# A two-block fp32 transformer on one Trainium2 core: row broadcast by memory reload replaced by small matmuls

## The chip, the cores and the metric

The kernel runs on one core of a Trainium2 chip. The metric is the time on the device in microseconds (us), the median of repeated runs; lower is better. Engines are named as in the profile: PE is the matmul engine, DVE the vector engine, ACT the scalar (activation) engine, POOL the general-purpose engine, SP the queue that loads weights.

## The reference, cut to what matters

Input is one sequence of 1024 tokens, 1024 wide, float32. The first block (differential and stick-breaking attention, then a gated FFN with a convolution) is not touched. The second block is touched between its input projection and its output projection:

```python
q_a,k_a,v_a,q_m,k_m,v_m,o_m,i_m,f_m,g_a,g_m = split(h @ w_in)
y_a = sliding_window_attention(rope(q_a), rope(k_a), v_a, sinks)      # 8 heads of 64, window 128
logf = log_sigmoid(f_m + b_f); b = cumsum(logf); ig = i_m + b_i       # mLSTM gates, 4 heads
m_t = max(b + m_prev, max(d_mat))                                     # running maximum, the stabilizer
scores = (q_m @ k_m) * exp(d_mat - m_t)                               # 4 heads of 128
h_m = (scores @ v_m) / max(abs(sum(scores)), exp(-m_t))
y_m = sigmoid(o_m) * head_layer_norm(h_m)
merged = sigmoid(g_a) * (y_a @ w_ba) + sigmoid(g_m) * (y_m @ w_bm)
mix = merged @ w_out
```

For each mLSTM head the kernel needs one row of 1024 numbers, minus the running maximum, repeated on all 128 partitions. Four rows become a 128 x 4096 array, called NEGMB. It also needs two small arrays with time along the partitions (GT and EMT, 128 x 32 each).

## The kernel before, in words

Feature dimension and partitions: activations are stored with 128 features on the partitions and the 1024 tokens along the row, in 8 tiles. Every large product is done in split precision: the activation is split in a high and a low part (`hh`, `hl`), each weight chunk (128 x 1024) too (`wh`, `wl`), and one 128 x 128 x 512 product takes three matmuls (lines 546 to 548). Products of q, k, v and the like are plain float32; the profile shows each as two matmul records.

Weights go through a fixed ring: SP loads a chunk into `raw`, POOL makes `wh` (line 492, a cast) and `wl` (line 494, a subtraction), PE multiplies, and `chunk_done` tells POOL that the slot is free. There are three slots.

The order of the work in the second block is written out by hand for each engine:

1. 23 projection chunks of the input projection. Among them chunk 5 gives the gate rows, from which DVE and ACT make, in `ROW1` and `ROW2` (4 partitions each), the rows of the stabilizer. At n == 8 DVE negates the running maximum (`if_ch` 8); at n == 10 ACT writes it to the memory scratch `m_scratch` (lines 1599 to 1601).
2. Eight gate chunks, m = 8 to 15, first half of the tokens (`gate_product(..., 0)`). ACT copies each result out and stores it. After m = 9 it reloads `m_scratch` into NEGMB, repeated over 128 partitions (line 1621). Ahead of m = 12, PE runs `stabilizer_columns()`, 16 matmuls of 4 rows by 4 columns (lines 975 and 977), which ACT copies into GT and EMT after its copy of m = 12 (lines 1624 and 1625).
3. The mLSTM steps, s = 0 to 7: `m_scores` (line 1015), `m_values` (line 1027), with DVE adding the mask (`m_diag`, line 2315) and weighing the scores (line 2332), and ACT the exponentials.
4. The window attention, n = 0 to 7 and three steps to drain: `w_scores` (lines 1049 and 1052), row maxima on DVE (2384 to 2387), exponentials on ACT (1709, 1712), `w_turn` transposes (1063), `w_values` (1076).

The second half of the gate chunks, 16 chunks of 8 products, is used as filler of stages 3 and 4: `gate_fill(count)` does the next `count` products (three matmuls each), and a table says how many go where. ML_FILL gives 11 in each of 8 mLSTM steps (88), SW_FILL gives 5, 5, 6, 6, 6, 6, 6 in the window steps n = 0 to 6 (40). When a chunk's eighth product is done, ACT copies it through the single stage buffer G_STAGE (`gate_out`, line 1632), and POOL is set free for the split of a later chunk. Step n = 7 and the drain have no filler. In a window step with four transposes, filler products stand after each transpose; the last product stands behind the last transpose.

After stage 4 comes the branch projection; it first waits for the mLSTM half of its input.

Of the kernel before, what the change touches and what calls it, by code (L numbers as in the profile page):

```python
# [116 lines left out]
def build(nc, A):  # L117
    ctx = ExitStack()
    with ctx:
# [68 lines left out]
        m_row m_mb m_tp m_tpc m_S m_d m_E m_A m_pv m_U l_mu l_den l_sq l_v l_rs l_s l_y l_hi l_lo so_in0 so_in1 so_in2 so_in3  # L188
# [8 lines left out]
        m_dram = nc.dram_tensor("m_scratch", (HD_ML, S), F32, kind="Internal").ap()  # L197
# [184 lines left out]
        M_JUNK, G_STAGE = hhf[:, 6, 2 * P:3 * P], hhf[:, 7, 0:HALF]  # L382
# [25 lines left out]
        ML_FILL, SW_FILL = (3, 3, 3, 2), (5, 5, 6, 6, 6, 6, 6)  # L408
        assert ML_N * sum(ML_FILL) + sum(SW_FILL) == 8 * N_GATE
# [132 lines left out]
        def _(pe):  # L542
# [427 lines left out]
            def stabilizer_columns():  # L970

                pe.wait_ge(Z.if_ev, N_PROJ)
                pe.wait_ge(Z.if_act, 4)
                for b in range(NB):
                    pe.matmul(bank(2)[:, b * 4:b * 4 + 4], ROW1[0:4, b * P:(b + 1) * P], mat("ident")[0:4, 0:4],
                              start=True, stop=True)
                    last = pe.matmul(bank(3)[:, b * 4:b * 4 + 4], ROW2[32:36, b * P:(b + 1) * P],
                                     mat("ident")[32:36, 32:36], start=True, stop=True)
                last.then_inc(Z.m_tp, 1)

            pe.wait_ge(Z.v_cp, 10)
            for m in range(N_EARLY, N_GATE):
                pe.wait_ge(Z.split_done, C_GATE0 + m + 1)
                if m == N_EARLY + 2:
                    pe.wait_ge(Z.if_ev, N_PROJ - 2)
                if m >= N_EARLY + 4:
                    pe.wait_ge(Z.g_ev, m - 3)
                if m == N_EARLY + 4:
                    stabilizer_columns()
                for k in range(KT):  # L990
                    last = gate_product(G_BANKS[m % 4], C_GATE0 + m, k, 0)
                last.then_inc(Z.chunk_done, 1)
# [15 lines left out]

            pe.wait_ge(Z.m_tpc, 2)
# [129 lines left out]
        def _(act):  # L1139
# [412 lines left out]
            for n in range(N_PROJ):  # L1552
# [52 lines left out]
            for m in range(N_EARLY, N_GATE):  # L1605
# [11 lines left out]
                if m == N_EARLY + 1:  # L1617
                    act.wait_ge(Z.m_row, 16)
                    act.wait_ge(Z.sg_out0, 32)
                    act.wait_ge(Z.rope_done, 5)  # L1620
                    act.dma_start(NEGMB, bass.AP(m_dram.tensor, 0, [[0, P], [S, HD_ML], [1, S]])).then_inc(Z.m_mb, 16)
                if m == N_EARLY + 4:
                    act.wait_ge(Z.m_tp, 1)
                    act.activation(GT, bank(2)[:, 0:32], ACT.Copy).then_inc(Z.m_tpc, 1)
                    act.activation(EMT, bank(3)[:, 0:32], ACT.Copy).then_inc(Z.m_tpc, 1)

            def gate_out(c):

                act.wait_ge(Z.chunk_done, C_GATE1 + c + 1)
                if c:  # L1630
                    act.wait_ge(Z.gs4, 16 * c)
                act.activation(G_STAGE, bank(6 + c % 2), ACT.Copy).then_inc(Z.g_ev, 1)
# [3 lines left out]
            act.wait_ge(Z.chunk_done, C_GATE1)  # L1636
            act.wait_ge(Z.m_mb, 16)
            act.wait_ge(Z.m_tpc, 2)
            act.wait_ge(Z.sg_out1, 32)
            for strip_out in (Z.gs0, Z.gs1, Z.gs2, Z.gs3):  # L1640
                act.wait_ge(strip_out, 16 * ((N_GATE - N_EARLY) // 4))

# [87 lines left out]
            done = 0  # L1730
# [119 lines left out]
        def _(dve):  # L1850
# [408 lines left out]
            for n in range(N_PROJ):  # L2259
# [49 lines left out]
            dve.wait_ge(Z.chunk_done, C_GATE1)  # L2309
            def m_diag(s):  # L2310
# [6 lines left out]
            dve.wait_ge(Z.m_mb, 16)  # L2317
# [285 lines left out]
```

## Time and profile before

| quantity | value |
|---|---|
| median of 3 runs | 2996.53 us (2994.82 to 2996.93) |
| the profiled execution, its own time | 2996.93 us |
| its span, first to last instruction | 2995.1 us |
| mean granted PE clock | 0.978 of full |
| PE busy | 2868.9 us, 96% |
| DVE, ACT, POOL busy | 1556.7, 794.8, 1092.7 us |

In the profile, "idle before" is the time an engine stood still ahead of an instruction, with the instruction that ended it. A matmul's end is modelled, so that matmuls overlap in the listing; the distance between starts is what one costs. PEclk is the granted clock as a share of 2.4 GHz; 0.50 is 1.2 GHz.

### The profile page before, as it was taken

To read this page: it belongs to the slowest core of one execution; us is meant where nothing else is said; L and a number is where in the kernel's file an instruction comes from. 1 tells how busy PE (TensorE), PEld (TensorE's weight loads), DVE (VectorE), ACT (ScalarE), POOL (GpSimd) and SP (SyncE) were. 2 spreads that over 40 slices of the span, in tenths; PEclk is the share of its full clock that TensorE was granted. 3 is DMA by queue.
4 is the path that set the end of the run, shared out by engine and by line. 5 is a ranking of instruction groups with operands and counts; after the bars stand their busy time and mean duration, and the time that the engine had idled before them with its cause. 6 is when DMAs were issued, how large, how long until landed. Compare 5 with 4: busy or idle time off the path is not lost.

```text
span 2995.1 us, 36945 instructions
## 1 busy us (share of the span) xinstructions
PE 2868.9 (96%) x13558; PEld 2283.5 (76%) x13558; DVE 1556.7 (52%) x2118; ACT 794.8 (27%) x1534; POOL 1092.7 (36%) x626
## 2 busy tenths in 40 slices
PE   7999999899899999999899999998999999999997
PEld 5767777677788888887688887766787888888885
DVE  3665577738556556557734303473446344344346
ACT  4544444434111111112413114553232000000002
POOL 2555412445233333335432343221364333333333
PEclk9999999999999999999999999997999999999998
DMA  3322222032111111112411332212432111111112
GB/s 115 101 81 83 85 78 69 17 120 85 49 43 48 49 49 49 49 49 78 154 64 49 84 141 94 80 43 81 161 98 72 49 49 49 49 47 44 49 63 99
DMA packets 62777, 218.39 MB, mean 73 GB/s; under 512 B 6831, under 2 KB 8144, under 8 KB 62292
## 3 DMA queue, kind: packets, MB, share of 16 engines
q1 hardware_dynamic: 47120, 169.89, 17.3%
q10 hardware_dynamic: 15556, 47.12, 4.5%
q8 instruction: 68, 1.11, 0.2%
q14 instruction: 33, 0.27, 0.0%
HBM read 194.68 MB, written 19.68 MB: 72 GB/s over the span
## 4 chain that ended last, share of the span: by engine, by line
PE 84%; DVE 10%; ACT 3%; issue 2%; DMA 0%; ACTq 0%; POOL 0%; DVEq 0%
PE ps L546 24%; PE ps L547 24%; PE ps L548 24%; PE ps L633 2%; PE ps L653 2%; PE ps L667 1%; DVE ps L1902 1%; PE ps L1027 1%; PE ps L1015 1%; PE ps L670 1%; DVE ps L1885 1%; DVE arena L2043 1%; DVE ps L1926 1%; DVE dsm L2025 1%; PE ps L1049 1%
## 5 line engine op out<-in xcount | busy, mean ns | idle before, releaser
L492 POOL CAST wh<-raw 128x1024 fp32r<-128x1024 f32 x272 | 290.4, 1068 | 1720.8 <-PE ps L548 1697.3
L546 PE MATMUL ps<-hh,wh 128*128 128x512 f32 x1968 | 799.5, 406 | 15.1 <-DVE hl L1858 5.2
L547 PE MATMUL ps<-hl,wh 128*128 128x512 f32 x1968 | 772.7, 393 | 0.0
L548 PE MATMUL ps<-hh,wl 128*128 128x512 f32 x1968 | 772.6, 393 | 0.0
L494 POOL TENSOR_TENSOR wl<-raw,wh 128x1024 fp32r<-128x1024 f32 x272 | 654.5, 2406 | 21.8
L546 PEld LDWEIGHTS ps<-hh,wh 128*128 128x128 f32 x1968 | 374.0, 190 | 103.9 <-issue 17.3
L548 PEld LDWEIGHTS ps<-hh,wl 128*128 128x128 f32 x1968 | 373.1, 190 | 80.5
L547 PEld LDWEIGHTS ps<-hl,wh 128*128 128x128 f32 x1968 | 374.4, 190 | 73.8 <-issue 3.4
L2103 DVE TENSOR_TENSOR hlf<-ps,hlf 128x512 f32<-128x512 f32 x288 | 196.0, 692 | 321.8 <-PE ps L548 321.8
L546 PE MATMUL ps<-ah,wh 128*128 128x512 f32 x832 | 327.4, 394 | 5.6 <-DVE al L1917 3.1
L548 PE MATMUL ps<-ah,wl 128*128 128x512 f32 x832 | 324.4, 390 | 0.0
L547 PE MATMUL ps<-al,wh 128*128 128x512 f32 x832 | 324.3, 390 | 0.0
L546 PE MATMUL ps<-gated,wh 128*128 128x512 f32 x704 | 276.7, 393 | 15.9 <-DVE arena L2132 15.4
L548 PE MATMUL ps<-gated,wl 128*128 128x512 f32 x704 | 275.4, 391 | 0.0
L547 PE MATMUL ps<-gated,wh 128*128 128x512 f32 x704 | 275.4, 391 | 0.0
L2103 DVE TENSOR_TENSOR arena<-ps,arena 128x512 f32<-128x512 f32 x288 | 196.0, 692 | 126.9 <-PE ps L548 126.9
L546 PEld LDWEIGHTS ps<-ah,wh 128*128 128x128 f32 x832 | 156.5, 188 | 42.7 <-DVE al L1917 5.8
L547 PEld LDWEIGHTS ps<-al,wh 128*128 128x128 f32 x832 | 156.6, 188 | 33.3 <-issue 1.2
L548 PEld LDWEIGHTS ps<-ah,wl 128*128 128x128 f32 x832 | 156.5, 188 | 32.7
L546 PEld LDWEIGHTS ps<-gated,wh 128*128 128x128 f32 x704 | 133.2, 189 | 46.0 <-issue 8.5
L518 POOL TENSOR_TENSOR arena<-arena 128x1023 f32<-128x1023 f32 (+7 forms) x64 | 122.6, 1924 | 115.6 <-DVE arena L2015 61.5
L547 PEld LDWEIGHTS ps<-gated,wh 128*128 128x128 f32 x704 | 133.2, 189 | 27.7 <-issue 0.2
(259 smaller groups left out, 3062.8 us busy)
## 6 DMA issues: line engine op xcount, KB each, us to landing
raw<-weights SPq DMA_DIRECT2D x272, 512.0 KB, 3.3
arena<-w_ada SPq DMA_DIRECT2D x48, 512.0 KB, 3.8
arena<-gate_scratch ACTq DMA_DIRECT2D x20, 512.0 KB, 5.5
arena<-x_t ACTq DMA_DIRECT2D x1, 4096.0 KB, 14.0
gate_scratch<-arena ACTq DMA_DIRECT2D x16, 256.0 KB, 2.3
x_scratch<-arena ACTq DMA_DIRECT2D x1, 4096.0 KB, 13.1
gate_scratch<-hhf ACTq DMA_DIRECT2D x16, 256.0 KB, 2.0
hhf<-x_scratch ACTq DMA_DIRECT2D x1, 4096.0 KB, 15.4
```

Of the source, the lines that this page charges most:

```text
L492: pool.tensor_copy(wh[:, s], raw[:, r]).then_inc(Z.wt_hi, 1)
L494: pool.tensor_tensor(wl[:, s], raw[:, r], wh[:, s].bitcast(F32), ALU.subtract).then_inc(Z.split_done, 1)
L518: pool.tensor_tensor(beta[:, 0:w], beta[:, 0:w], S_U[u % 3][:, 1:w + 1], ALU.mult).then_inc(Z.s_a, 1)
L546: pe.matmul(out, wh[:, slot, w], xh, start=start, stop=False)
L547: pe.matmul(out, wh[:, slot, w], xl, start=False, stop=False)
L548: return pe.matmul(out, wl[:, slot, w], xh, start=False, stop=stop)
L633: last = pe.matmul(bank(2 * side, 2)[:, c:e], Q_T[i % 2][r, query(s)], K_T[i % 2][r, c:e], start=True, stop=(i >= SB_JOBS), skip_group_che ...
L653: last = pe.transpose(bank(4)[:, (k - lo) * P:(k - lo + 1) * P], src[:, k * P:(k + 1) * P], mat("ident"))
L667: last = pe.matmul(bank(5)[r, 0:P], HV[i % 2][:, k, r], S_AT[side][s % 2][:, kt], start=(k == 0), stop=(k == b), skip_group_check=True)
L670: last = pe.matmul(bank(5)[:, 0:P], HV[i % 2][:, k], D_WT[s % 2][:, kt], start=(k == 0), stop=(k == b))
L1015: pe.matmul(bank(M_SBANK[s % 3])[:, lo:], T(9 + h)[:, k * P:(k + 1) * P], T(5 + h)[:, c * HALF + lo:(c + 1) * HALF], start=True, stop=True ...
L2103: dve.tensor_tensor(t, bank(4 + o % 4), t, ALU.add).then_inc(Z.dn_free, 1)
```

## The change

NEGMB is no longer made by a store to memory and a repeated reload. It is made by 8 matmuls: a selection matrix M_SEL (4 partitions, minus one in the column block of its head) times the row of the running maximum gives a 128 x 512 piece in banks 0 and 1 by turns, and ACT copies each out. M_SEL is made by 4 DVE instructions once the first-half gate chunks are done. The 16 small matmuls of the stabilizer columns move from ahead of m = 12 to behind the 8 new matmuls. Two filler products stand before the first new matmul and one behind each, 10 in all; they are taken from the window steps, which get 5 in each of n = 0 to 5 and none at n = 6. These matmuls and fillers make a new stage between 2 and 3. M_SEL shares its place with G_STAGE, so the first `gate_out` waits until the 8 new matmuls are done.

```diff
-        ML_FILL, SW_FILL = (3, 3, 3, 2), (5, 5, 6, 6, 6, 6, 6)
+        PRE_FILL, ML_FILL, SW_FILL = (2,) + 8 * (1,), (3, 3, 3, 2), 6 * (5,)
...
-                if m == N_EARLY + 4:
-                    stabilizer_columns()
...
+            gate_fill(PRE_FILL[0])
+            pe.wait_ge(Z.if_ev, N_PROJ)
+            pe.wait_ge(Z.m_sel, 1)
+            pe.wait_ge(Z.if_act, 4)
+            for h in range(HD_ML):
+                for half in range(2):
+                    i = 2 * h + half
+                    if i >= 2:
+                        pe.wait_ge(Z.m_mbc, i - 1)
+                    pe.matmul(bank(i % 2), M_SEL[32:36, h * P:(h + 1) * P], ROW1[32:36, half * HALF:(half + 1) * HALF],
+                              start=True, stop=True).then_inc(Z.m_mb, 1)
+                    gate_fill(PRE_FILL[1 + i])
+            for b in range(NB):
...
+            last.then_inc(Z.m_tp, 1)
+            pe.wait_ge(Z.m_mbc, 8)
             pe.wait_ge(Z.m_tpc, 2)
...
-                if n == 10:
-                    act.wait_ge(Z.if_ch, 8)
-                    act.dma_start(m_dram, ROW1[32:36, :]).then_inc(Z.m_row, 16)
...
-                    act.dma_start(NEGMB, bass.AP(m_dram.tensor, 0, [[0, P], [S, HD_ML], [1, S]])).then_inc(Z.m_mb, 16)
...
+            for i in range(8):
+                act.wait_ge(Z.m_mb, i + 1)
...
+                act.activation(NEGMB[:, i // 2, (i % 2) * HALF:(i % 2 + 1) * HALF], bank(i % 2), ACT.Copy).then_inc(Z.m_mbc, 1)
+            act.wait_ge(Z.m_tp, 1)
+            act.activation(GT, bank(2)[:, 0:32], ACT.Copy).then_inc(Z.m_tpc, 1)
+            act.activation(EMT, bank(3)[:, 0:32], ACT.Copy).then_inc(Z.m_tpc, 1)
...
-                    dve.wait_ge(Z.if_ch, 7)
-                    gate_rows(dve.tensor_scalar(ROW1[32:36, :], ROW1[32:36, :], -1.0, None, ALU.mult))
...
             dve.wait_ge(Z.chunk_done, C_GATE1)
+            for h in range(HD_ML):
+                ins = dve.tensor_scalar(M_SEL[32:36, h * P:(h + 1) * P], mat("ident")[32:36, 32 + h:33 + h].to_broadcast([4, P]),
+                                        -1.0, None, ALU.mult)
+            ins.then_inc(Z.m_sel, 1)
...
-            dve.wait_ge(Z.m_mb, 16)
+            dve.wait_ge(Z.m_mbc, 8)
```

## Rows read from the trace of the kernel before

**Rows 1.** The page: each engine's busy time

```profile
PE 2868.9 (96%) x13558; PEld 2283.5 (76%) x13558; DVE 1556.7 (52%) x2118; ACT 794.8 (27%) x1534; POOL 1092.7 (36%) x626
```

**Rows 2.** Windows at the first-half gate chunks; columns as in the first line

```profile
core 0: us, PE busy (x) PEld busy (x) DVE busy (x) ACT busy (x) POOL busy (x), PEclk, DMA share, GB/s
1756.00:1777.62 21.62, 21.62 (x97) 17.70 (x95) 0.00 (x0) 4.11 (x5) 13.72 (x8) 1.00 0.66 233
1777.62:1779.60 1.98, 1.98 (x34) 1.87 (x33) 0.00 (x0) 0.60 (x1) 1.30 (x2) 1.00 0.71 257
1779.60:1787.00 7.40, 7.40 (x27) 5.94 (x26) 0.00 (x0) 0.00 (x0) 2.11 (x1) 0.77 0.28 104
```

**Rows 3.** Timeline of ACT there: start, duration, instruction

```profile
1768.02 0.38 ACTq L1621 DMA_DIRECT2D arena<-m_scratch  x1
...
1777.82 0.60 ACT L1614 ACTIVATE arena<-ps 128x512 f32<-128x512 f32 x1 [4.84 <-PE ps L548]
...
1787.00 0.60 ACT L1614 ACTIVATE arena<-ps 128x512 f32<-128x512 f32 x1 [8.58 <-PE ps L548]
...
1788.01 0.20 ACT L1624 ACTIVATE small<-ps 128x32 f32<-128x32 f32 x1 [0.40 <-ACT arena L1614]
1788.10 0.19 ACT L1625 ACTIVATE small<-ps 128x32 f32<-128x32 f32 x1
1792.44 0.60 ACT L1614 ACTIVATE arena<-ps 128x512 f32<-128x512 f32 x1 [4.15 <-PE ps L548]
```

**Rows 4.** Chain that ended last, start of the mLSTM steps

```profile
1803.29 0.86 PE ps L1015 x2
```

**Rows 5.** PE's groups by line: a 33-row and a 128-row matmul, duration

```profile
L685 PE MATMUL ps<-arena x8: 482/520/587, 105.4 to 132.0; 33*128 33x384 f32 x8
...
L1015 PE MATMUL ps<-arena 128*128 128x384 f32 x2 | 0.8, 484 | 0.0
```

**Rows 6.** Timelines of DVE and POOL at that start

```profile
1803.33 1.34 DVE L2315 TENSOR_TENSOR hhf<-arena,mats 128x128 f32<-128x128 f32 x2 [81.80 <-PE ps L548]
...
1803.48 1.04 POOL L492 CAST wh<-raw 128x1024 fp32r<-128x1024 f32 x1 [1.87 <-PE ps L548]
1804.60 2.39 POOL L494 TENSOR_TENSOR wl<-raw,wh 128x1024 fp32r<-128x1024 f32 x1
```

**Rows 7.** Timeline of DVE: four column scalings twice, a small subtraction once

```profile
1897.21 1.11 DVE L2359 TENSOR_SCALAR arena<-arena,dsm,small 128x128 f32<-128x128 f32 x4
...
1950.87 2.19 DVE L2387 TENSOR_TENSOR wsm<-cols,wsm 128x4 f32<-128x4 f32 x1
...
1970.17 3.23 DVE L2359 TENSOR_SCALAR arena<-arena,dsm,small 128x128 f32<-128x128 f32 x4
```

**Rows 8.** Windows at the window attention's steps and drain; columns as in rows 2

```profile
2008.36:2021.02 12.66, 12.59 (x92) 8.84 (x91) 6.90 (x15) 6.95 (x25) 1.56 (x1) 1.00 0.19 63
2021.02:2033.82 12.80, 8.70 (x73) 5.79 (x73) 6.90 (x15) 7.22 (x26) 3.40 (x2) 0.96 0.18 61
2033.82:2044.83 11.01, 7.99 (x48) 6.15 (x48) 4.77 (x8) 3.93 (x7) 0.00 (x0) 0.50 0.01 2
```

**Rows 9.** Timeline of PE: scores, transposes, values; ACT's last exponential

```profile
1955.17 1.23 PE L1049 MATMUL ps<-arena 64*128 64x256 f32 x4 [3.99 <-ACT wsm L1712]
1962.56 1.05 PE L1063 MATMUL ps<-mats,arena 128*128 128x128 f32 x4
...
2012.62 1.97 PE L1076 MATMUL ps<-arena 128*64 128x128 f32 x32
...
2019.76 0.63 PE L1063 MATMUL ps<-mats,arena 128*128 128x128 f32 x4
...
2020.41 0.21 ACT L1712 ACTIVATE wsm<-wsm 128x4 f32<-128x4 f32 x1
...
2032.42 0.64 PE L1063 MATMUL ps<-mats,arena 128*128 128x128 f32 x4 [0.78 <-ACT arena L1717]
...
2033.82 3.68 PE L1076 MATMUL ps<-arena 128*64 128x128 f32 x32 [0.77 <-ACT arena L1717]
```

More of the change, by code:

```diff
@@ L196, in build @@
         x2_dram = nc.dram_tensor("x2_scratch", (P, KT * S), F32, kind="Internal").ap()
-        m_dram = nc.dram_tensor("m_scratch", (HD_ML, S), F32, kind="Internal").ap()
         sg_dram = nc.dram_tensor("gate_scratch", (20, P, S), F32, kind="Internal").ap()
@@ L381, in build @@
         M_D = [hhf[:, 6, 0:P], hhf[:, 6, P:2 * P]]
-        M_JUNK, G_STAGE = hhf[:, 6, 2 * P:3 * P], hhf[:, 7, 0:HALF]
+        M_JUNK, M_SEL, G_STAGE = hhf[:, 6, 2 * P:3 * P], hhf[:, 7, 0:HALF], hhf[:, 7, 0:HALF]
         M_A = [hhf[:, 0:4, 0:HALF], hlf[:, :, 0:HALF]]
@@ L406, in build @@
         W_STEPS = ML_N + NB + 3
-        ML_FILL, SW_FILL = (3, 3, 3, 2), (5, 5, 6, 6, 6, 6, 6)
-        assert ML_N * sum(ML_FILL) + sum(SW_FILL) == 8 * N_GATE
+        PRE_FILL, ML_FILL, SW_FILL = (2,) + 8 * (1,), (3, 3, 3, 2), 6 * (5,)
+        assert sum(PRE_FILL) + ML_N * sum(ML_FILL) + sum(SW_FILL) == 8 * N_GATE
         def gates_done(before, count):
@@ L968, in _ @@
                 tile((C_IN + n) % SL, 2 * (n % 3), SPLIT_H)
[L970 to L979, printed above, removed]
             pe.wait_ge(Z.v_cp, 10)
@@ L1006, in gate_fill @@
                 gates_filled[0] += count
+            gate_fill(PRE_FILL[0])
[11 more added lines that the diff above has]
+            for b in range(NB):
+                pe.matmul(bank(2)[:, b * 4:b * 4 + 4], ROW1[0:4, b * P:(b + 1) * P], mat("ident")[0:4, 0:4],
+                          start=True, stop=True)
+                last = pe.matmul(bank(3)[:, b * 4:b * 4 + 4], ROW2[32:36, b * P:(b + 1) * P],
+                                 mat("ident")[32:36, 32:36], start=True, stop=True)
+            last.then_inc(Z.m_tp, 1)
+            pe.wait_ge(Z.m_mbc, 8)
             pe.wait_ge(Z.m_tpc, 2)
@@ L1631, in gate_out @@
                     act.wait_ge(Z.gs4, 16 * c)
+                else:
+                    act.wait_ge(Z.m_mb, 8)
                 act.activation(G_STAGE, bank(6 + c % 2), ACT.Copy).then_inc(Z.g_ev, 1)
@@ L1634, in gate_out @@
                 act.dma_start(sg_dram[HD_ML + c][:, half_of(1)], G_STAGE).then_inc(Z.gs4, 16)
-            act.wait_ge(Z.chunk_done, C_GATE1)
-            act.wait_ge(Z.m_mb, 16)
+            for i in range(8):
+                act.wait_ge(Z.m_mb, i + 1)
+                if i == 0:
+                    act.wait_ge(Z.sg_out0, 32)
+                    act.wait_ge(Z.rope_done, 5)
+                act.activation(NEGMB[:, i // 2, (i % 2) * HALF:(i % 2 + 1) * HALF], bank(i % 2), ACT.Copy).then_inc(Z.m_mbc, 1)
+            act.wait_ge(Z.m_tp, 1)
+            act.activation(GT, bank(2)[:, 0:32], ACT.Copy).then_inc(Z.m_tpc, 1)
+            act.activation(EMT, bank(3)[:, 0:32], ACT.Copy).then_inc(Z.m_tpc, 1)
+            act.wait_ge(Z.m_mbc, 8)
             act.wait_ge(Z.m_tpc, 2)
@@ L1641, in _ @@
                 act.wait_ge(strip_out, 16 * ((N_GATE - N_EARLY) // 4))
+            for c in gates_done(0, sum(PRE_FILL)):
+                gate_out(c)
             def m_weights(steps):
@@ L1728, in w_high @@
                 act.activation(hh[:, 0:4, n * P:(n + 1) * P], bank(5).rearrange("p (j q) -> p j q", j=4), ACT.Copy).then_inc(Z.w_hi, 1)
-            done = 0
+            done = sum(PRE_FILL)
             for s in range(W_STEPS):
```

10 lines of the change are left out of this document (1 added, 9 removed).

## The prediction

> **What bounds the kernel now.** I read the page first: PE is busy 96% of the span [rows 1], so at most places a microsecond of added PE work is a microsecond of time, and a microsecond that any other engine saves is worth nothing. The question is then what PE does at each place that the change touches. I read three places: the first-half gate chunks, where the reload runs, by windows and by ACT's timeline [rows 2, 3]; the start of the mLSTM steps, by the chain and by the timelines of DVE and POOL [rows 4, 6]; and the window attention, by windows and by PE's timeline [rows 8, 9]. The reader is to see that PE has no gap at the first two, and that the third is another regime: a step's length is the same with fillers and without.
>
> **What is removed.** The reload is issued at 1768.02 [rows 3]. From 1756.00 to 1777.62 PE is busy 21.62 of 21.62 us at a granted clock of 1.00 [rows 2], so neither the 2 MB nor their share of the DMA engines costs PE anything: removing them is worth 0. The work that hides them is the three gate chunks behind them. The DVE negation, the store at n == 10 and the two ACT waits lie beside projection matmuls in the same way: 0.
>
> The stabilizer block is worth something. ACT copies a gate chunk out when PE is done with it, so the distance of two copies is PE's time for a chunk. It is 1792.44 - 1787.00 = 5.44 us for 24 matmuls, 0.227 each and 0.68 for a product of three. Across the block it is 1787.00 - 1777.82 = 9.18 us, 3.74 more [rows 3]. Of these, 1.98 us are the block itself (1777.62 to 1779.60), and the rest, 1.76 us, comes right behind it, where the granted clock has a mean of 0.77 [rows 2]: full-size matmuls run for a while at the lower level, 1.2 GHz. So ahead of the mLSTM steps the change gives back 3.74 us.
>
> **What is added on PE, ahead of the mLSTM steps.**
> - Ten filler products: 10 x 0.68 = 6.80 us.
> - Eight matmuls of 4 rows by 512 columns. None is in the trace. The nearest row for the length is a float32 matmul of 128 rows and 512 columns, 0.86 us [rows 4]. Does it get cheaper with 4 rows instead of 128? A record of 33 rows and 384 columns has a median of 520 ns, one of 128 rows a mean of 484 [rows 5], so rows don't count, and I take 8 x 0.86 = 6.88 us. The lower bound, if 4 rows were to overlap wholly with the fillers, is 0; the upper is 8 x 1.72 = 13.8 at the lower clock. It is nearest to 6.88.
> - The block of 16 small matmuls, moved: 1.98 us again.
> - The new wait at its end for ACT's copies. PE used to go on with m = 12 meanwhile; now everything queued behind the wait is the mLSTM scores, so PE stands still. Both copies take 1788.29 - 1788.01 = 0.28 [rows 3]; with the signals there and back I take 0.5 (bounds 0.3 to 1).
> - The clock behind the block. The block and the wait are a longer thin stretch than before, so I take the same loss again, 1.76 us (bounds 0 and 3.5, twice that).
>
> The sum is -3.74 + 6.80 + 6.88 + 1.98 + 0.50 + 1.76 = +14.18 us.
>
> The Trainium skill weighs on the second item ("TensorE: Matmul & The Clock Gate", section "Why this matters for your kernels"): a matmul of 32 rows takes as long as one of 128, and few rows pay only if several that sit in different row groups are issued together. By that rule the sum stays as it is, since the eight all sit in partitions 32 to 35 and have a full-height filler between them; rows 5 agree on the first half of the rule.
>
> **The wait for M_SEL.** It could come late. DVE is set free by the same signal as before, at 1803.33, and has four instructions to do by the time PE has done two fillers, 1.36 us after 1803.13, at 1804.49. But POOL starts a split at 1803.48, and DVE's first two instructions took 1.34 us instead of twice 0.28 or so: the second stood until the cast was over, at 1804.52. The subtraction follows at 1804.60 for 2.39 us [rows 6]. What DVE does under such a subtraction can be seen elsewhere: a four-element operation took 2.19 us, and four column scalings, the same kind of instruction as M_SEL's, took 3.23 instead of 1.11 [rows 7]. If M_SEL's last instructions slip in before 1804.60, PE waits about 0.3 us; if they stand until 1806.99, they end at about 1807.5 and PE waits 3.0. Scalings cost 0.28 each here (1.11 / 4), so four don't fit: I hold the late case slightly the likelier, 0.55.
>
> The Trainium skill has a page on it ("SBUF — State Buffer", section "SBUF: two separate sides"): DVE and POOL share one pair of ports as an exclusive lock, and the loser waits for the whole instruction. By that rule the wait is 3.0 rather than something between; rows 7 agree with it.
>
> ACT's eight copies (0.60 each, [rows 3]) are hidden behind matmul and filler (0.86 + 0.68 = 1.54), and PE waits for the copy of two pieces before. They would cost about 0.2 us apiece without the fillers.
>
> **What the window attention gives back.** It has ten fillers fewer, 6.8 us of PE work. But a step there is a chain: scores, row maxima, exponentials, then transposes with ACT's copies between them. In step 6, with six fillers, the last transposes start at 2019.76, 11.40 us after the step (2008.36). In step 7, with none, they start at 2032.42, again 11.40 after 2021.02 [rows 8, 9]. So a filler between the transposes is free, and taking one out saves 0. Only the one behind the last transposes could count; it stays in steps 2 to 5. In step 6 it goes: the scores of step 7 could start when the last exponential is done, 2020.62, and not at 2021.02 [rows 9]. That is -0.4, and with a signal's delay -0.3.
>
> **The clock there.** Where fillers are gone the PE is thin. Step 7, without fillers, ends with the clock falling: its mean is 0.96, and the next window is at 0.50 throughout [rows 8]. Now step 6 is such a step too. If the clock falls at its end, step 7 starts at 1.2 GHz. Its scores then take 1962.56 - 1955.17 = 7.39 us as in step 2, instead of 2012.62 - 2008.36 = 4.26, which is +3.13. Its values take 3.68 instead of 1.97, +1.71 [rows 9]. Both are on the chain: together +4.84. The drain behind it is at 0.50 anyway. I give this 0.6.
>
> **Sum.** The part without doubts is 14.18 - 0.3 = +13.9. Two things on top are each likelier than not: +3.0 for M_SEL (0.3 if not, left out) and +4.8 for the clock. Exactly one of them: 0.55 x 0.4 + 0.45 x 0.6 = 0.49, at +16.9 or +18.7. Both: 0.33, at +21.7. None: 0.18, at +13.9. I forecast one of them, about +18. The profiled execution took 2996.93 us, of which 2995.1 is the span; it is within 0.4 us of the median, 2996.53. So 2996.5 + 18 = 3014.5 us, 0.6% slower.
>
> **The rivals.**
> - *The window steps do follow their PE work.* Then all ten fillers come back, -6.8 instead of -0.3, and with no loss to the clock it is +14.18 - 6.8 = +7.4, 3003.9 us. For it: in step 6 PE is busy 12.59 of 12.66. Against it: the 11.40 twice. 0.07.
> - *The new stage runs at the lower clock.* It is half 4-row matmuls, and a block of 4-row matmuls is what the clock fell behind. If all of its 6.80 + 6.88 us run at 1.2 GHz, that costs up to 13.7 more, beside the +13.9; in half of it, +7. For it: rows 2. Against it: half of the work is full fillers, the share that step 6 has too, at 1.00. Above +27, 0.10.
> - *Not slower: the PE clock stays up in the drain.* All of the drain's values run at 0.50 now. If the thin stretch falls so that the clock is up again for the three blocks of values, that is 3 x 1.71 = 5.1; with the five groups of transposes and the start of the branch projection, some 4 more. Then +13.9 - 9 = +5, 3001.4 us, within 0.2%. It decides only if at least 8 us of that come. For it: only that the clock's timing is not tied to the work. Against it: the stretch gets thinner, not denser. 0.05.
> - *The change does nothing to the path*, since the eight matmuls overlap with fillers (-6.88) and the fillers come back whole: +14.18 - 6.88 - 6.8 = +0.5, 2997 us. 0.02.
>
> **How the numbers follow.** One or none or both of the two doubtful costs, up to +27: 0.76; the others as above. The subtraction can also hit other DVE operations in the mLSTM steps now, as the chunks end two fillers earlier there; one hit is 2.2 us [rows 7], either way. The range from +7 to +27.5 takes in the first rival, the case without either cost less two such hits, and both costs with the lower clock twice as long behind the block and one hit. It leaves out the other rivals, 0.17: 3003.5 to 3024 us. A measurement of this kernel tells from no change about 0.2%, 6 us. Faster by more than that, 0.03; within, 0.06; slower, 0.91.
>
> **What would show it.** In the profile after: first-half gate chunks all 5.44 us apart, no drop of the clock there; eight matmuls of 4 rows 1.54 us apart, 0.86 of it theirs; a PE idle of about 3 us in front of the first with DVE as its end, or none; the window steps 3 to 5 as long as now, 13 us; step 7 with scores of 7.4 us or 4.3. The mLSTM steps start some 12 to 15 us later. I am wrong in the mechanism if the window steps shorten by 0.6 each, or if the total is within 6 us of the time before.

## The result and the profile after

The changed kernel takes 3024.43 us (median of 4 runs, 3022.54 to 3025.32) against 2995.68 us for the kernel before on the same chip: a ratio of 1.0098, interval 1.0083 to 1.0114, 0.98% slower. The forecast was 3014.5 us, +18 instead of the +28.7 of the medians; 3024.4 lies just above its range. The profiled execution of the changed kernel took 3021.23 us, with a span of 3019.5.

PE is busy for 18.4 us more than in [rows 1], and the span is 24.4 us longer:

```profile
PE 2887.3 (96%) x13574; PEld 2287.1 (76%) x13574; DVE 1554.7 (51%) x2121; ACT 799.8 (26%) x1542; POOL 1091.9 (36%) x626
```

To place the 24.4 us I cut both traces at the same events. "Gates" runs from ACT's table load ahead of the first-half gate chunks to the start of its copy of m = 15, "new stage" from there to the first mLSTM scores, then mLSTM to the first window scores, window attention to the first branch projection, and the rest:

| us | until the gates | gates | new stage | mLSTM | window | rest | span |
|---|---|---|---|---|---|---|---|
| before | 1757.5 | 45.8 | -0.2 | 132.2 | 125.9 | 933.8 | 2995.1 |
| after | 1754.7 | 42.0 | 32.1 | 131.5 | 126.3 | 932.8 | 3019.5 |
| difference | -2.8 | -3.7 | +32.3 | -0.7 | +0.4 | -1.0 | +24.4 |

Of what was changed, the first column holds only the DVE negation and the store that were removed. Over all the traces here it lies between 1753.5 (e9, which keeps both) and 1759.1 (e8, which has neither), so some us of a total are chance.

Windows of the changed kernel over the gates, the two fillers and the first broadcast, the rest of the broadcasts, the block of small matmuls with its wait, and the start of the mLSTM steps (columns as in [rows 2]):

```profile
1754.80:1796.60 41.80, 41.80 (x187) 34.59 (x186) 0.00 (x0) 5.43 (x8) 26.19 (x15) 1.00 0.42 146
...
1796.60:1800.30 3.70, 3.46 (x13) 1.74 (x11) 1.47 (x4) 1.20 (x2) 3.27 (x2) 1.00 0.52 199
1800.30:1824.85 24.55, 24.55 (x37) 9.09 (x36) 0.49 (x2) 4.18 (x7) 3.58 (x3) 0.51 0.13 43
1824.85:1828.90 4.05, 3.57 (x33) 3.52 (x33) 0.00 (x0) 0.35 (x3) 0.00 (x0) 0.50 0.00 0
1828.90:1834.00 5.10, 5.10 (x10) 3.42 (x11) 0.89 (x2) 2.14 (x5) 0.00 (x0) 0.50 0.14 53
```

The reader is to see three things. Where the block stood, the clock is 1.00 all through, and the drop of [rows 2] is gone. From the second broadcast on, PE is busy 24.55 of 24.55 us and at 0.51: no idle time led to it but the 0.24 us ahead of the first broadcast. And it stays at 1.2 GHz through the block and into the mLSTM steps.

Timeline of PE in the new stage: the first broadcast with its filler, the second, and two further on; then the first mLSTM scores.

```profile
1798.36 1.09 PE L1004 MATMUL ps<-arena,hhf 4*128 4x512 f32 x2 [0.24 <-issue]
1799.38 0.50 PE L545 MATMUL ps<-hh,wh 128*128 128x512 f32 x1
...
1800.27 1.58 PE L1004 MATMUL ps<-arena,hhf 4*128 4x512 f32 x2
...
1803.37 2.07 PE L1004 MATMUL ps<-arena,hhf 4*128 4x512 f32 x2
1805.37 0.80 PE L545 MATMUL ps<-hh,wh 128*128 128x512 f32 x1
...
1806.94 2.07 PE L1004 MATMUL ps<-arena,hhf 4*128 4x512 f32 x2
...
1828.90 2.05 PE L1020 MATMUL ps<-arena 128*128 128x512 f32 x2 [0.48 <-ACT small L1639]
```

A broadcast with its filler takes 1.91 us once (1798.36 to 1800.27), then 3.10, then 3.57. The forecast had 1.54 for each. The first broadcast waited 0.24 us, so the 3 us for a late M_SEL did not come. Timelines of DVE and POOL there:

```profile
1796.79 1.47 DVE L2314 TENSOR_SCALAR hhf<-mats 4x128 f32<-4x128 f32 x4 [78.07 <-PE ps L547]
...
1796.95 1.09 POOL L491 CAST wh<-raw 128x1024 fp32r<-128x1024 f32 x1 [1.87 <-PE ps L547]
1798.12 2.36 POOL L493 TENSOR_TENSOR wl<-raw,wh 128x1024 fp32r<-128x1024 f32 x1
```

In the window attention, the timeline of PE in step 6 (scores, last transposes) and step 7 (scores, values), to be read beside [rows 9]:

```profile
2034.37 0.70 PE L1054 MATMUL ps<-arena 64*128 64x256 f32 x4
...
2045.76 0.63 PE L1068 MATMUL ps<-mats,arena 128*128 128x128 f32 x4 [0.78 <-ACT arena L1722]
2046.67 1.22 PE L1054 MATMUL ps<-arena 64*128 64x256 f32 x4 [0.28 <-ACT wsm L1717]
```

The last transposes start 11.39 us after the step, now without fillers between; [rows 9] had 11.40 with them. Step 7 starts 12.30 after step 6 instead of 12.66. And its scores run at the lower clock, 1.22 instead of 0.70 us for a group.

### The profile page after: what moved, and what is told of

Same layout as the page of the kernel before. It is cut to its first block, busy times and chain, and to the rows that moved or that the text cites. A ratio compares the mean times of both kernels' runs of the same rounds, so it can differ in the third digit from the quotient of the medians.

```text
span 3019.5 us, 36986 instructions
## 1 busy us (share of the span) xinstructions
PE 2887.3 (96%) x13574; PEld 2287.1 (76%) x13574; DVE 1554.7 (51%) x2121; ACT 799.8 (26%) x1542; POOL 1091.9 (36%) x626
## 4 chain that ended last, share of the span: by engine, by line
PE 84%; DVE 10%; ACT 3%; issue 2%; DMA 0%; POOL 0%; ACTq 0%; DVEq 0%
PE ps L545 24%; PE ps L547 24%; PE ps L546 24%; PE ps L632 2%; PE ps L652 2%; DVE ps L1907 1%; PE ps L666 1%; PE ps L1032 1%; PE ps L1020 1%; DVE arena L2048 1%; DVE ps L1890 1%; PE ps L669 1%; DVE dsm L2030 1%; PE ps L1054 1%; DVE ps L1931 1%
## 5 line engine op out<-in xcount | busy, mean ns | idle before, releaser
L545 PE MATMUL ps<-gated,wh 128*128 128x512 f32 x704 | 277.1, 394 | 14.8 <-DVE arena L2137 14.8
```

What stands on the lines that cost most here:

```text
L545: pe.matmul(out, wh[:, slot, w], xh, start=start, stop=False)
```

## The experiments

All are against the kernel before on the same chip. "Full height" means that a matmul reads 128 partitions. In the table, stages are cut as above (e10 is described under its own heading; e11 and e12 are second traces of e1 and e2); each stage number is from one trace, each ratio from several executions.

| run | median us | ratio (interval) | gates | new stage | mLSTM | window | span |
|---|---|---|---|---|---|---|---|
| e1_rows128 | 3013.09 | 1.0058 (1.0041 to 1.0075) | 42.0 | 16.6 | 128.6 | 128.6 | 3004.7 |
| e2_reload_kept | 3001.11 | 1.0012 (1.0003 to 1.0022) | 42.0 | 9.0 | 129.0 | 125.6 | 2994.0 |
| e3_block_early | 3022.39 | 1.0089 (1.0072 to 1.0105) | 45.8 | 27.7 | 130.4 | 125.6 | 3018.7 |
| e4_burst | 3020.18 | 1.0081 (1.0064 to 1.0098) | 42.0 | 23.4 | 128.7 | 128.6 | 3011.5 |
| e5_spread | 2996.03 | 1.0003 (0.9994 to 1.0012) | 46.3 | -0.2 | 132.2 | 125.4 | 2993.9 |
| e6_block_128rows | 2993.96 | 0.9999 (0.9989 to 1.0008) | 48.9 | -0.2 | 132.3 | 121.2 | 2992.3 |
| e7_two_fillers | 3019.76 | 1.0082 (1.0066 to 1.0097) | 42.0 | 25.0 | 133.9 | 127.1 | 3017.5 |
| e8_rows128_no_fill | 3006.85 | 1.0034 (1.0020 to 1.0047) | 42.0 | 11.3 | 134.0 | 127.4 | 3007.3 |
| e9_two_ahead | 2989.57 | 0.9981 (0.9972 to 0.9990) | 44.2 | 1.2 | 128.6 | 125.9 | 2986.8 |
| e10_rows128_two_ahead | 3003.26 | 1.0025 (1.0015 to 1.0034) | 42.0 | 11.3 | 130.5 | 127.1 | 2999.9 |
| e11_rows128_again | 3014.84 (one) | | 42.0 | 16.6 | 128.7 | 133.3 | 3013.0 |
| e12_reload_again | 2998.00 (one) | | 42.0 | 9.0 | 129.1 | 125.8 | 2996.2 |

### Full-height broadcasts: e1_rows128

The selection matrix gets zeros in the other 124 partitions, and both operands are read over all 128; the same numbers are added up. Matmuls, fillers and copies are as many as before.

```diff
-    pe.matmul(bank(i % 2), M_SEL[32:36, h * P:(h + 1) * P], ROW1[32:36, half * HALF:(half + 1) * HALF],
+    pe.matmul(bank(i % 2), M_SEL[:, h * P:(h + 1) * P], ROW1[:, half * HALF:(half + 1) * HALF],
...
-                ins = dve.tensor_scalar(M_SEL[32:36, h * P:(h + 1) * P], mat("ident")[32:36, 32 + h:33 + h].to_broadcast([4, P]),
+                ins = dve.tensor_scalar(M_SEL[:, h * P:(h + 1) * P], mat("ident")[:, 32 + h:33 + h].to_broadcast([P, P]),
```

> The eight broadcast matmuls read all 128 rows instead of 4 (the other 124 rows of the selection are zero); nothing else changes. Theory A, the clock fell because 4-row matmuls are thin work for the array: the new stage, from the last first-half gate chunk to the first mLSTM scores, takes 16 to 19 us instead of 32.3, at full clock up to the small block; about 14 us come off, ratio to before 1.003 to 1.006. Theory B, the clock fell because of float32 matmuls and the small stops in front of them, whatever their height: the stage stays at 30 to 33 us and the ratio near 1.009.

The new stage went from 32.1 to 16.6 us, and the total from 1.0098 to 1.0058. Windows over the broadcasts, and PE's timeline of two of them:

```profile
1800.30:1812.50 12.20, 12.20 (x44) 7.27 (x42) 0.16 (x1) 4.79 (x8) 4.43 (x3) 1.00 0.15 44
```

```profile
1801.34 1.02 PE L1004 MATMUL ps<-arena,hhf 128*128 128x512 f32 x2
...
1802.89 1.02 PE L1004 MATMUL ps<-arena,hhf 128*128 128x512 f32 x2
```

With more partitions at work and nothing else changed the clock stays at 1.00, and a pitch is 1.55 us, the 1.54 of the forecast. So the low height of the broadcasts is what the clock falls on. In the total the full height gives back 0.40%, 12 us, and not the 15.5 us of the stage and the 2.9 of the mLSTM steps: the window attention takes 2.3 us more than in the changed kernel in this trace, and 7.0 in the next.

This trace was of the fastest of four executions (3006.5; the others 3011.5 to 3014.8 at a lower mean clock). The difference might have been a fall of the clock in the very stage. A second trace was taken:

> The kernel with the broadcasts over 128 rows once more, for a second trace. Its first trace was of the fastest of four executions: 3006.5 us at a mean granted clock of 0.981, the others 3011.5 to 3014.8 at 0.975 or 0.976. If the others lose their 5 to 8 us in the new stage (the clock falls there too, for a part of it), the stage is 21 to 25 us in this trace instead of 16.6, and rows at work are only a part of the cause. If it is 16.6 again and the total is above 3011, the clock fell elsewhere, and the stage tells rightly of the rows.

It took 3014.84 us, and the new stage was 16.6 us again, with all pitches at 1.55. Of the 8.3 us that the span is longer, 2.7 lie ahead of the gates, 0.9 behind the window attention, and 4.7 in it (133.3 against 128.6 us), in its drain. The windows from some 21 us behind the start of step 7 to the end, of the first trace and of the second:

```profile
2052.00:2071.90 19.90, 11.01 (x106) 8.53 (x102) 8.09 (x10) 10.62 (x15) 0.00 (x0) 0.91 0.00 1
```

```profile
2055.00:2079.40 24.40, 15.46 (x105) 11.73 (x101) 7.87 (x10) 10.68 (x15) 0.00 (x0) 0.57 0.00 1
```

The same work at 0.91 and at 0.57, 19.9 and 24.4 us: there one kernel differs from one execution to the next.

### Without broadcasts: e2_reload_kept

The reload stays; only the ten fillers and the block are moved. Shown against the changed kernel, cut:

```diff
-                    pe.matmul(bank(i % 2), M_SEL[32:36, ...], ROW1[32:36, ...], ...).then_inc(Z.m_mb, 1)
                     gate_fill(PRE_FILL[1 + i])
```

> The broadcast goes back to the store and reload through memory; the ten fillers and the small block stay where the change put them. This prices the moved pieces alone: -3.7 ahead of the stage, 6.8 for ten fillers, 2 for the block, 0.5 for the wait, 1.8 to 3.5 for the clock behind the block. Theory A (only the broadcasts are to blame for the low clock): stage 9 to 11 us with the clock up until the block, about +7 us over before, ratio 1.002 to 1.003. Rival (moving fillers out of the window steps costs much by itself, by the clock in step 7): +12 us or more, ratio above 1.004.

Ratio 1.0012, about +3.5 us, stage 9.0 us: 6.8 of fillers, the block and the wait. A second trace was taken of it too, since its first was of its shortest execution:

> The kernel with the reload kept and the ten fillers and the block moved, once more, for a second trace. Its first was at 2995.8 us and a clock of 0.982; most of the others had 2999 to 3004 at 0.977 to 0.979. It has no broadcast. If the 3 to 8 us between executions lie in the clock behind the block or in the window attention, they are in those stages here too, and a stage without broadcasts stays at 9.0 us; if the stage itself is longer than 9.0 by some us, fillers and block alone can lose the clock there.

Stage 9.0, mLSTM 129.1, window 125.8: as in the first, 2.2 us longer in all, 2.0 of them ahead of the gates. The clock was not lost in the stage in either trace. Most executions of e2 took 2998.7 to 3001.8 us, those of the two traces 2995.8 and 2998.0; where the others lose the difference was not seen, so fillers and block may lose some clock in them. Of the 28.7 us (3024.43 - 2995.68), all but some 3.5 (0.9 to 6.6 by the interval) come with the broadcasts.

### The block back in its place: e3_block_early

```diff
+                if m == N_EARLY + 4:
+                    stabilizer_columns()
...
-            for b in range(NB):
-                (the block of 16 small matmuls behind the broadcasts)
```

> Only the 16 small matmuls and their two copies go back ahead of the fifth gate chunk; broadcast matmuls and fillers as in the change. Theory A: the stage still falls to 1.2 GHz behind the first broadcasts, loses the block's 3.6 us and the 0.5 of the wait: 27 to 29 us instead of 32.3, and the 3.7 us ahead of it come back: total within 2 us of the change. Rival (the block behind the broadcasts keeps the clock down): the stage gets much shorter, below 22 us.

The ratio is 1.0089 against 1.0098, intervals overlapping: where the block stands hardly matters. The clock falls in the stage without it:

```profile
1808.00:1829.00 21.00, 21.00 (x30) 7.63 (x29) 0.00 (x0) 3.37 (x6) 3.40 (x2) 0.50 0.09 32
```

### Broadcasts in one go: e4_burst

```diff
-PRE_FILL, ML_FILL, SW_FILL = (2,) + 8 * (1,), (3, 3, 3, 2), 6 * (5,)
+PRE_FILL, ML_FILL, SW_FILL = (2,) + 7 * (0,) + (8,), (3, 3, 3, 2), 6 * (5,)
```

> The eight broadcast matmuls stand in one run behind the first two fillers, and the other eight fillers behind them, instead of one after each. Theory A: the run of 4-row matmuls alone takes the clock down, at 1.0 to 2.0 us each 8 to 16 us, and the eight fillers behind it bring it up again after some 3 to 4 us: stage 22 to 28 us, shorter than the change's 32.3, ratio 1.005 to 1.008. Rival (a mixture of half fillers is no worse than a run): the stage stays at 32 us or gets longer.

PE's timeline, the eight broadcasts and the filler behind them:

```profile
1799.59 10.88 PE L1004 MATMUL ps<-arena,hhf 4*128 4x512 f32 x16 [0.24 <-issue]
1810.40 0.80 PE L545 MATMUL ps<-hh,wh 128*128 128x512 f32 x1
```

They take 10.81 us (at full clock 8 x 0.86 would be 6.9). The clock falls in the course of them, as the windows show:

```profile
1799.59:1802.90 3.31, 3.31 (x8) 1.21 (x8) 0.00 (x0) 1.57 (x3) 2.11 (x1) 1.00 0.24 76
1802.90:1810.40 7.50, 7.50 (x11) 2.50 (x9) 0.00 (x0) 2.61 (x5) 0.00 (x0) 0.50 0.21 68
```

In the first window the matmul records start mostly 0.43 us apart, two to a broadcast: 0.86, what 128 rows cost too. But fewer fillers are caught by the low clock: 23.4 us of stage instead of 32.1, and 0.17% in the total, with intervals that overlap.

### Two fillers to a broadcast: e7_two_fillers

```diff
+PRE_FILL, ML_FILL, SW_FILL = (0,) + 8 * (2,), (3, 3, 3, 2), 6 * (4,)
```

> The changed kernel with two fillers behind each 4-row broadcast instead of one, none ahead of the first, and four instead of five in each window step. If two fillers are enough to keep the clock up, a pitch is about 0.9 + 1.36 = 2.3 us and the stage 8 x 2.3 + 3 = 21 to 22 us, 10 less than the changed kernel's 32.1 though it holds six fillers more: ratio to the kernel before about 1.006. If the clock falls all the same, a pitch is 3.58 + 1.36 = 4.9 us and the stage about 43 us: ratio about 1.013. In between: it falls later or comes back in part.

The stage is 25.0 us with six fillers more. The window over all eight, and two starts:

```profile
1799.39:1819.88 20.49, 20.49 (x63) 10.51 (x64) 0.30 (x2) 4.80 (x8) 5.53 (x3) 1.00 0.19 63
```

```profile
1801.99 1.12 PE L1004 MATMUL ps<-arena,hhf 4*128 4x512 f32 x2
1803.04 0.50 PE L545 MATMUL ps<-hh,wh 128*128 128x512 f32 x1
...
1804.62 1.12 PE L1004 MATMUL ps<-arena,hhf 4*128 4x512 f32 x2
```

The clock holds at 1.00. So here one full filler per 4-row broadcast is too little and two are enough, and a 4-row broadcast has a price at full clock too: the pitch is 2.63, less two fillers (1.36) 1.27 us, where a full-height one costs 1.55 - 0.68 = 0.87. The 0.40 are at the changes of height, to 4 rows and back: the filler does not start until 1.05 behind the broadcast, and between broadcasts of 4 rows alone (e4) nothing of the kind is seen. The total is only 0.16% better than the changed kernel, with overlapping intervals, since 6 x 0.68 = 4.1 us more of fillers stand ahead, PE waits 1.6 us for M_SEL where no filler covers it, and the mLSTM steps take 2.4 more than in the changed kernel.

### Full height without fillers: e8_rows128_no_fill

The broadcasts are at full height as in e1; the diff shows what else differs.

```diff
-PRE_FILL, ML_FILL, SW_FILL = (2,) + 8 * (1,), (3, 3, 3, 2), 6 * (5,)
+PRE_FILL, ML_FILL, SW_FILL = 9 * (0,), (3, 3, 3, 2), (5, 5, 6, 6, 6, 6, 6)
```

> The kernel with the broadcasts over 128 rows at full clock, and with the ten fillers back in the window steps (none in the new stage). My theory is that a filler in a window step is free and one in the new stage costs its 0.68: then the stage is 16.6 - 6.8 = about 10 us instead of 16.6 (eight broadcasts at 0.86 to 1.0, block 2, wait 0.5), the window attention stays at 126 to 128.5, and the ratio is 1.0058 - 0.0022 = about 1.0035. Rival: the fillers give back in the window what they cost ahead: ratio unchanged at 1.0058. Second rival: broadcasts back to back wait for ACT's copies, which take 0.6 each behind them, and the pitch is 1.5 all the same: stage 16 us.

The ratio came out at 1.0034, as forecast, but not by the working behind it. PE's timeline and the window over the eight:

```profile
1802.67 7.39 PE L1004 MATMUL ps<-arena,hhf 128*128 128x512 f32 x16 [1.61 <-issue]
```

```profile
1802.67:1809.99 7.32, 7.32 (x16) 2.43 (x17) 0.00 (x0) 4.18 (x7) 2.11 (x1) 1.00 0.28 102
```

Eight in 7.32 us, 0.91 each, at 1.00, beside 10.81 for the same number with 4 rows. ACT's copies set no pace. But PE waits 1.61 us for M_SEL: that is what two fillers hid. And the mLSTM steps are 134.0 us, 5.4 more than in e1; in them the clock is at 1.2 GHz for two stretches, the first right behind the block (3.58 us at 0.52), where it has 1.00 all through in e1. Beside the second trace of e1 (span 3013.0) this one (3007.3) has -5.3 in the stage, +5.4 in the mLSTM steps and -5.8 in the window attention; beside the first it is longer. What the fillers cost by themselves is better read from e10 below.

### Which fillers help the mLSTM steps: e9_two_ahead, e10_rows128_two_ahead

The mLSTM steps took 128.6 to 129.1 us at full clock with ten fillers ahead, and 132 to 134 with none or sixteen. Ten is two more than a chunk of eight.

```diff
 (e9, against the kernel before)
-        ML_FILL, SW_FILL = (3, 3, 3, 2), (5, 5, 6, 6, 6, 6, 6)
+        PRE_FILL, ML_FILL, SW_FILL = 2, (3, 3, 3, 2), (5, 5, 5, 5, 6, 6, 6)
...
+            gate_fill(PRE_FILL)
             pe.wait_ge(Z.m_tpc, 2)
```

> The kernel before with one thing changed: two of the filler products stand ahead of the first mLSTM scores, and two of the window steps have five fillers instead of six. With ten fillers ahead, the kernels so far had mLSTM steps of 128.7 to 129.0 us at full clock, with none or 16 of them 132.2 to 134.1 (kernel before: 132.3). Ten is two more than a chunk of eight. Theory: what counts is where the chunk ends, so two do what ten do: the new stretch costs 2 x 0.68 = 1.4, the mLSTM steps take 3.3 less, the window attention is unchanged; net -1.9 us, ratio 0.9994. Rival: the 3.3 us came of the moved block or the missing reload; then +1.4 us, ratio 1.0005, and the mLSTM steps stay at 132.3.

128.6 us instead of 132.2: two do what ten do. The ratio is 0.9981, faster than both kernels by more than the uncertainty; that is -5.7 us where I had expected -1.9. PE's waits over the gates, mLSTM and window stages that changed, of the kernel before and then of this one:

```profile
PE ps L1015 <- DVE hlf L2332: 2.4, 1, 2.4
...
PE ps L1027 <- ACT small L1672: 1.1, 1, 1.1
```

```profile
PE ps L1016 <- DVE hlf L2333: 1.9, 2, 1.4
```

Windows over the stretch of that wait, before and in this one:

```profile
1880.00:1890.00 10.00, 7.63 (x27) 5.39 (x28) 6.06 (x12) 3.67 (x12) 1.46 (x1) 0.83 0.15 53
```

```profile
1880.00:1890.00 10.00, 10.00 (x56) 7.94 (x55) 4.32 (x10) 5.94 (x27) 3.42 (x2) 1.00 0.20 71
```

A wait of PE of 2.4 us in one piece, with the clock at 0.83 around it, is gone; the waits listed are 1.9 us instead of 3.5, and the clock is at 1.00 all through the mLSTM steps. In this trace the block ahead of m = 12 also lost no clock. ACT's copies of m = 11 and 12 are 7.57 us apart instead of the 9.18 of [rows 3]:

```profile
1773.81 0.60 ACT L1615 ACTIVATE arena<-ps 128x512 f32<-128x512 f32 x1 [4.84 <-PE ps L548]
...
1781.38 0.60 ACT L1615 ACTIVATE arena<-ps 128x512 f32<-128x512 f32 x1 [6.97 <-PE ps L548]
```

Nothing ahead of the block differs from the kernel before, so that the fall behind it is by all signs a matter of the execution. Whether this makes the rest of the -5.7 us is open.

e10 is e1 with two fillers ahead of the broadcasts, none between them, and the other eight back in the window steps.

> The broadcasts over 128 rows, with two filler products ahead of them, none between, and the other eight back in the window steps. Theory: the two hide the 1.6 us in which PE stood in front of the first broadcast without them, so the stage stays at 11.3 us (9.7 + 1.4 + 0.2), and the mLSTM steps take 129 to 130 instead of 134.1 us; sum against the kernel with none ahead -4 to -5, ratio to the kernel before 1.002. Rival: the mLSTM steps keep 134: ratio 1.0034. It would be the best form of the change either way, and still slower than the kernel before.

Ratio 1.0025, stage 11.3, mLSTM 130.5: the best form of the change that was run, and 0.25% slower than the kernel before. That the mLSTM steps take 1.9 us more than in e1 is mostly the clock behind the block, which did not fall there in e1; it costs half of 3.5 us, some 1.7:

```profile
1808.66:1812.20 3.54, 3.54 (x7) 2.12 (x8) 0.89 (x2) 1.54 (x4) 0.00 (x0) 0.52 0.00 0
```

### The old block: e5_spread and e6_block_128rows

e5 is the kernel before with the 16 small matmuls as one pair ahead of each product of m = 12; e6 is the kernel before with the block in its place but at full height (and still 4 columns).

```diff
 (e5)
-                    stabilizer_columns()
...
+                    if m == N_EARLY + 4:
+                        stabilizer_pair(k)
 (e6; the second matmul of the pair likewise)
-                    pe.matmul(bank(2)[:, b * 4:b * 4 + 4], ROW1[0:4, b * P:(b + 1) * P], mat("ident")[0:4, 0:4],
+                    pe.matmul(bank(2)[:, b * 4:b * 4 + 4], ROW1[:, b * P:(b + 1) * P], mat("ident")[:, 0:4],
```

> The kernel before with one thing changed: the 16 small matmuls stand no longer as a block ahead of the products of m = 12, but as one pair ahead of each of its eight products. Theory (the clock falls when little is moved through the array for a while, and a pair between full products is too short for it): the pairs still cost 16 x about 0.12 = 1.9 us, the 1.76 us at the lower clock behind the block go, so the distance of the two gate copies goes from 9.18 to about 7.4, and the time is 1.8 us less than before, a ratio of 0.9994. Rival (a pair costs a switch of its own, since each has to wait for the pipeline to drain of full matmuls): the distance stays at 9 us or more and the ratio is 1.000 or above.

The rival was right. The clock stays at 1.00, but the copies are 9.66 us apart instead of 9.18. PE's timeline of one pair and the start of the next:

```profile
1776.74 0.27 PE L972 MATMUL ps<-mats,arena 4*128 4x4 f32 x1
...
1777.06 0.50 PE L546 MATMUL ps<-hh,wh 128*128 128x512 f32 x1
...
1777.95 0.27 PE L972 MATMUL ps<-mats,arena 4*128 4x4 f32 x1
```

1.21 us from pair to pair, 0.53 more than a product of 0.68; in the block a pair cost 1.98 / 8 = 0.25. The other 0.28 is the change of height, eight times.

> The kernel before with the 16 small matmuls reading all 128 partitions instead of 4 (still 4 columns each; what they compute is another sum, so the stabilizer columns are not the reference's). Theory A (rows of the array at work are what counts): the block lasts its 2 us, the clock stays at full level behind it, and the distance of the gate copies is about 7.4 instead of 9.18. Theory B (any row of matmuls with 4 columns is too thin, whatever the rows, as most of each is start and drain): the fall stays, 9.2. Total within 2 us of the kernel before either way.

(The identity has zeros in the added rows, so the sums are the same as before, other than the expectation says.) Theory B was right, and more than right: the copies are 12.26 us apart. Windows over the block to where the clock falls, and on:

```profile
1777.46:1780.05 2.59, 2.59 (x25) 2.59 (x24) 0.00 (x0) 0.60 (x1) 2.00 (x2) 1.00 0.74 258
1780.05:1786.56 6.51, 6.51 (x21) 5.45 (x21) 0.00 (x0) 0.00 (x0) 1.38 (x1) 0.50 0.29 94
```

Matmuls of 4 columns are thin whatever their height. And the block became longer, 1777.46 to 1781.72, 4.26 us instead of 1.98: the two matmuls of a pair, on partitions 0 to 3 and 32 to 35, ran at once with 4 rows and one after the other at full height. PE's timeline of the kernel before, and of this one:

```profile
1777.85 0.25 PE L975 MATMUL ps<-mats,arena 4*128 4x4 f32 x1
1777.86 0.25 PE L977 MATMUL ps<-mats,arena 4*128 4x4 f32 x1
```

```profile
1777.82 0.36 PE L975 MATMUL ps<-mats,arena 128*128 128x4 f32 x2
1778.04 0.36 PE L977 MATMUL ps<-mats,arena 128*128 128x4 f32 x2
```

That the total is unchanged all the same is, in this trace, the window attention, 121.2 us instead of 125.9, at a clock of 0.93 instead of 0.86; whether that comes with the block or by chance is not shown. (The medians of the chip, 2993.96 and 2996.61 us, would give 0.9991, which lies in the interval too.)

## Why the prediction was wrong

**The step that failed** is the price of the new stage. Its terms, 6.80 for the fillers, 6.88 for the broadcasts, 1.98 for the block and 0.50 for the wait, were all taken at 2.4 GHz: 16.2 us. It took 32.3. Full-height broadcasts take 16.8 for the same list (16.6 + 0.2), so as a sum at full clock it was right to 0.6 us. The other 15.5 us are what 4 rows cost in the stage: 26.49 us from the first broadcast to the block (1798.36 to 1824.85) where the second full-height trace has 12.59 (1802.45 to 1815.04), +13.9; and 4.05 for block and wait, where it has 2.43, +1.6. Of the 13.9, 8 x 0.40 = 3.2 is the change of height (e7) and the remainder, 10.7, the clock.

It was named: the rival "the new stage runs at the lower clock", with up to 13.7 us more, was given 0.10. The argument against it was "half of the work is full fillers, the share that step 6 has too, at 1.00". Step 6 does not bear on it. What stands between its fillers are scores of 64 rows and transposes of 128 rows, not matmuls of 4. The row that did bear on it was at hand, the fall behind the block of 4-row matmuls in [rows 2], and I used it for a fixed 1.76 us instead of a rule. The error also hid in "rows don't count", from [rows 5]: true for the length of a full-clock matmul by itself (in e4 the first records start 0.43 us apart, as those of 128 rows in e8 do), wrong by 0.40 for a broadcast between fillers, and wrong for the clock.

The Trainium skill ("TensorE: Matmul & The Clock Gate", section "Why this matters for your kernels") ties the loss of the clock to gaps in which PE stands idle between matmul bursts. By that rule nothing would fall here. The windows show the fall with PE busy 24.55 of 24.55 us (and 2.59 of 2.59 ahead of the fall in e6), so for matmuls of few rows or columns the measurement decides against it.

**The other steps.**
- Removed block: -3.74 forecast, -3.74 measured (42.04 against 45.78). Right in this trace; e9 shows that 1.6 of it is there in some executions only. The move of the block as a whole was to cost 1.98 + 0.50 + 1.76 - 3.74 = +0.5; between e3 and the changed kernel it is 0.09% with overlapping intervals, not told from 0.
- Reload removed: 0 forecast. Right: e2 and e12, which keep it, have 42.0 us of gates, as e1 and the changed kernel have without it. The store and the negation lie ahead of the gates and were not tested alone.
- Clock behind the block: +1.76 forecast. The mLSTM steps are 131.5 us where e1 has 128.6: +2.9, since the clock came down earlier and was still down.
- M_SEL late, +3.0 at 0.55: it did not come, and the broadcast waited 0.24 us, near the 0.3 of the other case. Yet DVE was held up by POOL's cast as [rows 6] had it. The four instructions, and then the third and the fourth by themselves in DVE's timeline:

```profile
L2314 DVE TENSOR_SCALAR hhf<-mats x4: 209/214/1054, 1796.8 to 1798.0; 4x128 f32<-4x128 f32 x4
...
1797.07 1.05 DVE L2314 TENSOR_SCALAR hhf<-mats 4x128 f32<-4x128 f32 x1
...
1798.05 0.21 DVE L2314 TENSOR_SCALAR hhf<-mats 4x128 f32<-4x128 f32 x1
```

  The third took 1.05 us instead of 0.21 and ended at 1798.12, 0.08 behind the end of the cast (1798.04). The fourth started at 1798.05, ahead of the subtraction at 1798.12, and so was not held. The same is in all eight traces of kernels with M_SEL, at 4 and at 128 partitions. What was mis-sized is the 0.28 for an instruction, from which "four don't fit" followed: these start 0.14 us apart, so that two were in ahead of the cast and only one was left for the gap behind it. M_SEL is ready 1.6 us after the last chunk (e8), and the two fillers cover most of that. The Trainium skill ("SBUF — State Buffer", section "SBUF: two separate sides") has the port pair of DVE and POOL as a lock for a whole instruction, where the DVE instruction has two inputs or is in a mode that uses both port pairs. The trace agrees on the lock; the held instruction has one input, and no run shows its mode.
- Window steps: -0.3 forecast for ten fillers taken out, -0.36 measured for step 6, and the 11.40 us are 11.39 without fillers. Right for steps 3 to 6; steps 3 to 5 take 12.6, 13.5 and 12.7 us, before 13.0, 13.5 and 12.7, and with four fillers each (e7) 12.6, 13.5 and 12.7. Steps 1 and 2 are not such a chain by the same measure: in e7 they take 10.7 and 12.9 us where the changed kernel has 12.8 and 14.8, in part at a higher clock; why was not looked into. Against e1 the eight fillers that e10 puts back shorten the new stage by 5.3 us (16.6 to 11.3) and do not lengthen the window attention.
- Clock at step 7, +4.84 at 0.6: its scores did run at the lower clock (1.22 us for a group), and scores and values together took 10.67 us (2046.67 to 2057.34) instead of 6.15, +4.5. So the step as described came true. It was not paid in the sum, since the drain behind it, forecast at 0.50 "anyway", took 29.4 us instead of 34.1, -4.8, at 0.84 and 0.91:

```profile
2057.00:2068.00 11.00, 6.89 (x60) 5.46 (x56) 7.04 (x17) 7.95 (x25) 0.00 (x0) 0.84 0.01 2
2068.00:2086.70 18.70, 9.76 (x94) 7.69 (x93) 6.88 (x7) 10.12 (x15) 0.00 (x0) 0.91 0.00 1
```

  The rival "the clock stays up in the drain" was thus half right. With 1.0 us more in the steps ahead of step 6 and the -0.36, the window attention came to +0.4 us. The two traces of e1 show that this is not settled by the kernel.
- Not foreseen: the mLSTM steps get 3.6 us shorter, by PE's waits and by the clock, when the fillers ahead shift the ends of the chunks by two. e9 shows that the two fillers do it. That it is POOL's split of the next chunk that then no longer meets DVE's weighing of the scores is argued, not shown.

Added up over gates, stage and mLSTM steps: 14.2 forecast, +0.6 for the list at full clock, +15.5 for 4-row matmuls, +1.1 for the clock behind the block beyond its 1.76, and -3.6 in the mLSTM steps (132.2 to the 128.6 of e1) give 27.8; the traces have -3.7 + 32.3 - 0.7, 27.8 before rounding. The window attention adds 0.4, and the stages that were not changed take 3.8 off, which I hold for chance: the medians differ by 28.7. That the median lies only 0.4 us above the range is luck: a term 15.5 us too small stands beside a range kept wide for a late M_SEL, which did not come, and for step 7, which the drain paid back.

## What to carry to other kernels

Price a group of thin matmuls (few rows or few columns) by what it does to the clock of everything around it, not by its own length: look in the trace for the nearest thin group and read the granted clock behind it. If such work has to be done, use full height where zeros can fill the rows and it costs no more time by itself. To put it in one go rather than between full matmuls, where each change of height costs again, made the new stage 8.8 us shorter in e4, though the total could not be told from the changed kernel's. And moving filler work between stages changes when every later chunk ends: try a few counts, since two fillers moved (e9) gave 5.7 us, the one gain in this series.

## What the runs showed of the hardware

- The granted clock went from 2.4 to 1.2 GHz with PE busy all the time, when 4-row by 512-column float32 matmuls alternated with one full product (the changed kernel, e3) or stood alone (e4); it stayed up with two products between (e7), and with the same matmuls at 128 rows, alternating (e1, e11) or alone (e8, e10). It also fell in a block of 128-row matmuls of 4 columns (e6).
- Behind one and the same block of 16 small matmuls it fell in the kernel before and in e3, e7, e8 and e10 (there 3.54 us at 0.52), and not in e1, e2, e9, e11 and e12. In the drain of the window attention one kernel had 0.91 and 0.57 in two executions, 4.5 us apart.
- At full clock, back to back, a 4-row broadcast takes as long as one of 128 rows (records 0.43 us apart in e4 and e8). The changes from full height to 4 rows and back together cost 0.28 us (pairs of 4 columns) to 0.40 us (broadcasts).
- Two 4-row matmuls in partitions 0 to 3 and 32 to 35 start 0.01 us apart and run together (a pair in 0.25 us); at 128 rows the pair takes 0.45.
- A DVE tensor_scalar with one float32 input stood until a POOL cast was over, 1.05 us instead of 0.21, at 4 partitions as at 128 (1.06 in e1); one that started 0.08 us ahead of POOL's next instruction was not held.
